# Solved blocks packed and spread on VectorE, adaptive vectors summed on VectorE

## The chip, the cores and the metric

One core of a Trainium2 chip. The time of a run is what the device takes for one execution, in microseconds (us). Engines: TensorE (PE), VectorE (DVE), ScalarE (ACT), GpSimd (POOL) and SyncE (SP), which issues all the DMAs told of here. Each engine runs its own list of instructions in order and waits on semaphores for the others.

## What is computed

One layer of a hybrid diffusion block over 256 latent and 256 context tokens of width 1024. A normalised input, scaled and shifted by a conditioning vector, goes through one combined projection; branch A is a spatial-gating MLP, branch B a gated DeltaNet in both directions; both are merged, projected and added; then a grouped top-2 mixture of 16 experts follows. Two places matter here.

```python
def ada_params(cond, w_ada, b_ada):
    return jnp.split(jax.nn.silu(cond) @ w_ada + b_ada, 6, axis=-1)

m = jnp.where(strict, jnp.einsum('bhnik,bhnjk->bhnij', k_beta, k) * decay, 0.0)
t_inv = lax.linalg.triangular_solve(eye + m, eye, left_side=True, lower=True, unit_diagonal=True)
u_val = t_inv @ (v * beta)
w_key = t_inv @ (k_beta * jnp.exp(gc)[..., None])

def step(s, inp):
    a_n, u_n, w_n, qd_n, kd_n, gt_n = inp
    v_new = u_n - w_n @ s
    o_n = qd_n @ s + a_n @ v_new
    s = s * gt_n + jnp.einsum('bhck,bhcv->bhkv', kd_n, v_new)
    return s, o_n
```

The adaptive vectors are a product of one row of 1024 with a matrix of 1024 x 6144, and the inverse is that of a unit lower triangular matrix per head, direction and tile of tokens.

## The kernel before

**Pairs and tiles.** The 8 heads are worked in 4 pairs, i = 0 to 3. A pair has 2 heads, 2 directions and 4 tiles of 128 tokens: 16 triangular problems of 128 x 128. While pair i is inverted and scanned, the projections of the next pair j = i + 1 are made (convolution channels C0 to C5, dense columns D0 to D6, gate columns Z0 and Z1); beside the last pair it is branch A (PA0 to PA7). The work of all engines is ordered by hand, one list for each engine.

**The stream of weight halves.** Weights come as halves of 512 KB: SP's half(n) (L621) loads half n into one of HRING = 4 buffers and first waits until half n - 4 is released. A weight half is rounded by ScalarE (high, L1164) and the rest subtracted by VectorE (low, L1734), which releases it; ahead(m) does this two halves ahead of the one now used, and ScalarE's and VectorE's lists each have it. SP's after_split(m) (L668) loads the half that takes the buffer of half m + 2. An adaptive vector (numbers 0 to 7, 512 columns each) comes as four quarters of such halves; a quarter is released by the sum or product made of it (ada_taken). The order of all halves is fixed by PLAN. Call the quarters of vector 2i a0 to a3 and those of 2i + 1 b0 to b3. For pairs 0 to 2 the order of loading, which runs two halves ahead of PLAN's places, is C4 C5 a0-a3 D3 Z0 b0-b3 D4 Z1 D5 D6, then C0 and C1 of the next pair; beside the last pair it is PA5 a0-a3 PA6 PA7 b0-b3 PB0 (with a, b for vectors 6 and 7).

**The block solve.** VectorE writes the triangular matrices; SP's move_rows (L690) puts their rows into a DRAM tensor, move_blocks (L695) reads back the 16 x 16 diagonal blocks, and GpSimd inverts them (solve_blocks, L963). SP's move_solved (L702) stores the inverses, and their transposes, into the diagonals of two large DRAM tensors that were zeroed once, t_dram and u_dram; move_inverse (L708) reads corners of 64 columns from them, zeros and all, into u_by_lane and t_by_lane. write_zeros (L680) does the zeroing in 12 DMAs of 172 KB, and zeroes rows of the experts too.

**The levels.** TensorE's level_p (L2708) waits for u's corners, level_up (L2726) for t's. VectorE's masks (L1887) and updates come between, then quarter_p, quarter_up, last_p, last_copy (L1919), and place_last on ScalarE: the whole inverse.

**The scan.** Per pair four steps: TensorE solved(t), ScalarE new_value(t) (L1341), TensorE state_sum(t), VectorE new_state(t) (L1935, L1940), TensorE key_state(t + 1), VectorE residual(t + 1) (L1927), with state_query and step_out (L1948) beside them. TensorE fills between with the products of D3 to D6, Z0 and Z1 of the next pair; low and ahead of these halves stand between VectorE's steps. o_scale (L1349) and decay_exp then begin the next pair.

**The adaptive vectors.** TensorE's ada_chunk (L2872) multiplies quarters as they land, two per call, into bank 3; ScalarE copies the bank (ada_copy, L1384), TensorE adds the partial rows and the bias (ada_fold, L2886), ScalarE copies the row (L1392) and SP stores it.

Of the kernel before, what the change touches and what calls it, by code (L numbers as in the profile page):

```python
# [20 lines left out]
P = 128  # L21
D = 1024
# [73 lines left out]
def block_kernel(nc, x, c, ctx, c_ctx, w_ada, b_ada, norm1_g, norm2_g, w_in, a_ln_g, a_w_s, a_b_s,  # L96
# [3 lines left out]
    with stack:  # L100
# [17 lines left out]
        fold_bias = sb("fold_bias", [P, 8])  # L118
# [181 lines left out]
        ada_part = lane_part(26)  # L300
        ada_sums, ada_bias = ada_part[0:97, :], ada_part[P - 8:P, :]
        zeros = lane_part(6)
        blocks, raw_blocks = lane_part(12)[:, 0:256], lane_part(12)[:, 256:512]
# [34 lines left out]
        def tokens(at):  # L338
# [13 lines left out]
            "landed_ctx landed_x landed_small landed_gate landed_bias bias_room landed_conv landed_ab ident_ready squares_ready power_ready "  # L352
# [5 lines left out]
            "scores_ready decay_exp intra_exp m_ready intra_ready landed_zero landed_rows landed_blocks blocks_solved landed_solved "  # L358
            "p_sum p_masked up_sum u_updated inverse_placed "
            "step_ready ks_sum r_ready qs_sum qs_copied vnew_sum vnew_copied intra_sum o_part "  # L360
# [5 lines left out]
            "ada_taken ada_copied ada_folded ada_stored "  # L366
# [29 lines left out]
        row_dram, t_dram, u_dram = [nc.dram_tensor(name, (PROBLEMS * (P // BLOCK) * STRIP,), F32).ap()  # L396
                                    for name in ("problem_rows", "inverse_turned", "inverse")]
# [10 lines left out]
        def corner(t, b):  # L408

            whole = t.rearrange("(m x) -> m x", m=PROBLEMS)  # L410
            return whole[:, 4 * b * STRIP:4 * b * STRIP + 64 * P].rearrange("m (r k) -> r m k", r=64)[:, :, 0:HALF_BLOCK]
# [50 lines left out]
        for j in range(1, PAIRS):  # L462
# [67 lines left out]
        def dense_bank(n):  # L530
            return bank[2 if n > 24 and n % 2 else 3][:, 0:256]

# [84 lines left out]
        def _(sp):  # L617
# [46 lines left out]
            def store_ada(m):  # L664
                sp.wait_ge(s["side_copied"], SIDE_AT["ada", m] + 1)
                load(ada_dram[m * N:m * N + N].unsqueeze(0), ada_part[0:1, :], s["ada_stored"])
# [13 lines left out]
            def write_zeros():  # L680
                sp.wait_ge(s["ident_ready"], 3)
                for t in (t_dram, u_dram):
                    flat = t.rearrange("(p x) -> p x", p=P)
                    for n in range(6):
                        load(flat[:, n * 344:(n + 1) * 344], zeros[:, 0:344], s["landed_zero"])
# [9 lines left out]
            def move_blocks():  # L695
                sp.wait_ge(s["landed_rows"], 64 * i + 64)
                if i == 0:
                    sp.wait_ge(s["landed_zero"], 320)
# [46 lines left out]
            write_zeros()  # L745
            after_split(CHAN_AT[j, 2])
# [11 lines left out]
            sp.wait_ge(s["bias_room"], 1)  # L758
# [2619 lines left out]
```

## Time and profile before

| | |
|---|---|
| median of three runs | 862.99 us (861.13 to 866.02) |
| the profiled execution | 862.04 us |
| its span in the trace | 860.3 us |
| mean granted clock of TensorE | 0.973 |
| TensorE, VectorE, ScalarE, GpSimd busy | 775.3, 523.3, 423.0, 197.5 us |

The profile is of one execution. The span runs from the first instruction to the last; 1.7 us of the execution's time lie outside it. A granted clock of 1.00 is 2.4 GHz, 0.50 is 1.2 GHz. In the rows, L2512 is the line of the helper that issues nearly all matrix products, so the tile names tell the work apart. "[x <-y]" is the engine's idle time ahead of an instruction and what ended it; "issue" stands where the profile shows no waiting. A row of SP's is the time of issuing, not of the transfer.

### The profile page before, as it was taken

Reading aid. Unit: us, or ns where it says so; the run is one execution under the profiler, and the core shown is the slowest. Engines: PE = TensorE matmul, PEld = TensorE weight load, DVE = VectorE, ACT = ScalarE, POOL = GpSimd, SP = SyncE. Lnnn points to the kernel's source line nnn. Section 1 sums busy time; section 2 is a strip of 40 time slices with the busy share of each in tenths; the row PEclk is TensorE's granted clock in tenths of the full one; section 3 lists DMA queues with packets and bytes.
Section 4 is the critical chain, followed back from the end, with each engine's and each line's share of the span. In section 5 each row is a group of like instructions: output and inputs, shape, how many; then the busy total and the mean of one; then the engine's idle time right before and its main releaser. Section 6 shows DMA issues by size and latency. Waiting matters only on the chain.

```text
span 860.3 us, 15936 instructions
## 1 busy us (share of the span) xinstructions
PE 775.3 (90%) x6396; PEld 634.1 (74%) x6396; DVE 523.3 (61%) x780; ACT 423.0 (49%) x749; POOL 197.5 (23%) x362
## 2 busy tenths in 40 slices
PE   3998997999979999799779898998999999999975
PEld 1678886799858997599768778887777777687631
DVE  1488585457843578445564446668977675786143
ACT  3476653448425484245822445465666565673101
POOL 3003261103801137022230103011241223212201
PEclk9999998999989999899988999999999999999998
DMA  9969469535695366844867558863889999999992
GB/s 312 290 204 270 118 163 209 152 87 138 171 202 135 86 170 151 217 124 128 273 134 184 175 148 261 346 259 113 299 347 420 408 420 420 417 418 366 419 418 118
DMA packets 182021, 208.37 MB, mean 242 GB/s; under 512 B 50212, under 2 KB 155341, under 8 KB 169017
## 3 DMA queue, kind: packets, MB, share of 16 engines
q1 hardware_dynamic: 179833, 203.28, 72.8%
q0 software_dynamic: 2112, 4.04, 1.2%
q8 instruction: 52, 0.85, 0.4%
q14 instruction: 24, 0.20, 0.1%
HBM read 190.64 MB, written 20.22 MB: 245 GB/s over the span
## 4 chain that ended last, share of the span: by engine, by line
PE 59%; DMA 12%; DVE 10%; POOL 7%; issue 5%; ACT 4%; SPq 2%; POOLq 0%; ACTq 0%; DVEq 0%
PE bank L2512 57%; DMA raw<-in_w_e_dram 5%; POOL lane L980 3%; POOL lane L978 2%; SPq L619 2%; DVE w_lo L2197 2%; DMA half_raw<-in_w_in_dram 2%; PE bank L2515 2%; DMA lane<-problem_rows 2%; DMA problem_rows<-lane 1%; DMA raw<-in_w_ada_dram 1%; DVE chan L1833 1%; DVE half_lo L1737 1%; ACT lane L1292 1%; DMA mix_raw<-in_a_w_s_dram 1%
## 5 line engine op out<-in xcount | busy, mean ns | idle before, releaser
L2512 PE MATMUL bank<-hT,half_hi 128*128 128x256 f32 (+1 forms) x1024 | 226.6, 316 | 8.5 <-issue 4.8
L2512 PEld LDWEIGHTS bank<-hT,half_hi 128*128 128x128 f32 x1024 | 164.7, 189 | 24.5 <-issue 8.7
L2512 PE MATMUL bank<-hT,half_lo 128*128 128x256 f32 (+1 forms) x512 | 158.3, 309 | 0.0
L1737 DVE TENSOR_TENSOR half_lo<-half_raw,half_hi 128x1024 fp32r<-128x1024 f32 x88 | 108.3, 1231 | 50.3 <-ACT half_hi L1169 49.4
L2197 DVE TENSOR_TENSOR w_lo<-raw,w_hi 128x2048 fp32r<-128x2048 f32 x36 | 88.2, 2458 | 46.8 <-ACT w_hi L1602 46.8
L1169 ACT CAST half_hi<-half_raw 128x1024 fp32r<-128x1024 f32 x88 | 91.9, 1048 | 41.2 <-PE bank L2512 22.4
L2512 PEld LDWEIGHTS bank<-lane 64*64 64x64 f32 (+3 forms) x1968 | 82.0, 149 | 33.5 <-issue 19.6
L2512 PE MATMUL bank<-lane 64*64 64x64 f32 (+3 forms) x1968 | 90.3, 239 | 16.6 <-issue 12.7
L2512 PEld LDWEIGHTS bank<-hT,half_lo 128*128 128x128 f32 x512 | 97.1, 190 | 7.2 <-issue 1.9
L1602 ACT CAST w_hi<-raw 128x2048 fp32r<-128x2048 f32 x36 | 68.7, 1909 | 34.6 <-PE bank L2512 19.9
L1833 DVE SCALAR_TENSOR_TENSOR chan<-bank,conv_col,chan 128x508 f32<-128x508 f32 (+3 forms) x96 | 63.2, 658 | 10.3 <-ACT chan L1240 7.7
L955 POOL TENSOR_TENSOR lane<-v_nat,key_gates 128x256 f32<-128x256 f32 x32 | 25.1, 789 | 177.4 <-DVE lane L1935 156.2
L2512 PE MATMUL bank<-w_hi,window 128*128 128x512 f32 x192 | 63.6, 399 | 1.6 <-DVE w_lo L2197 1.6
L2512 PE MATMUL bank<-w_lo,window 128*128 128x512 f32 x192 | 62.0, 397 | 0.2 <-DVE w_lo L2197 0.2
L2512 PE MATMUL bank<-raw,narrow_window 128*64 128x256 f32 x448 | 51.8, 382 | 4.1 <-DMA raw<-in_w_e_dram 4.0
L2512 PEld LDWEIGHTS bank<-raw,narrow_window 128*64 128x64 f32 x448 | 31.0, 137 | 22.3 <-issue 4.6
L2197 DVE TENSOR_TENSOR w_lo<-raw,w_lo 128x2048 fp32r<-128x2048 f32 x18 | 42.5, 2363 | 5.9 <-ACT w_lo L1602 5.9
L2512 PEld LDWEIGHTS bank<-w_hi,window 128*128 128x128 f32 x192 | 36.1, 188 | 12.7 <-issue 4.5
L2512 PEld LDWEIGHTS bank<-w_lo,window 128*128 128x128 f32 x192 | 35.8, 188 | 8.7 <-DVE w_lo L2197 0.6
L1602 ACT CAST w_lo<-raw 128x2048 fp32r<-128x2048 f32 x18 | 34.4, 1910 | 11.0 <-PE bank L2512 7.7
L2512 PE MATMUL bank<-w_lo,act_hi 128*128 128x512 f32 x108 | 37.0, 397 | 0.0
L1068 POOL CAST window<-hT 128x2048 fp32r x8 | 19.5, 2434 | 58.0 <-PE bank L2512 37.2
(386 smaller groups left out, 1352.6 us busy)
## 6 DMA issues: line engine op xcount, KB each, us to landing
raw<-in_w_e_dram SPq DMA_DIRECT2D x96, 1024.0 KB, 10.8
half_raw<-in_w_in_dram SPq DMA_DIRECT2D x64, 512.0 KB, 5.0
half_raw<-in_w_ada_dram SPq DMA_DIRECT2D x32, 512.0 KB, 4.7
raw<-in_w_ada_dram SPq DMA_DIRECT2D x8, 1024.0 KB, 11.5
dense<-staged SPq DMA_DIRECT2D x32, 128.0 KB, 4.6
half_raw<-in_w_proj_a_dram SPq DMA_DIRECT2D x8, 512.0 KB, 5.9
half_raw<-in_w_proj_b_dram SPq DMA_DIRECT2D x8, 512.0 KB, 5.0
half_raw<-in_w_out_dram SPq DMA_DIRECT2D x8, 512.0 KB, 6.3
```

The source lines that it names most:

```text
L619: sp.dma_start(dst, src).then_inc(done, 16)
L955: last = pool.tensor_tensor(v_beta[pos % 2][:, :, d, :], v_nat[i % 2][:, :, t, :], key_gates[i % 2][:, KEY_BETA, t, :, d:d + 1].to_broadca ...
L978: own.after(pool.tensor_tensor(product_, y[:, k + 1:, k:k + 1].to_broadcast([P, rows_, cols_]), x[:, k:k + 1, 0:k + 1].to_broadcast([P, ro ...
L980: own.after(pool.tensor_tensor(x[:, k + 1:, 0:k + 1], x[:, k + 1:, 0:k + 1], product_, ALU.subtract))
L1068: pool.tensor_copy(window[q % 2][:, :, :, :], hT[:, :, :, bass.ds(at, P)].bitcast(F32))\
L1169: act.copy(half_hi[m % HBUF][:, :], half_raw[n % HRING][:, :]).then_inc(s["half_high"], 1)
L1602: act.copy(e_hi[k % WBUF][:, :], slots[n % SLOTS_AHEAD][:, :]).then_inc(s["hi_ready"], 1)
L1737: dve.tensor_tensor(half_lo[m % HBUF][:, :], half_raw[n % HRING][:, :], half_hi[m % HBUF][:, :].bitcast(F32), ALU.subtract).then_inc(s["ha ...
L1833: ins = dve.scalar_tensor_tensor(out=y[:, :, a:b], in0=ps[:, :, a + o:b + o], scalar=conv_col[:, CONV_KIND[n // 2], 2 * j + n % 2, tap:tap ...
L2197: dve.tensor_tensor(e_lo[k % WBUF][:, :], slots[n % SLOTS_AHEAD][:, :], e_hi[k % WBUF][:, :].bitcast(F32), ALU.subtract)\
L2512: return nc.tensor.matmul(dst, lhsT, rhs, start=start, stop=stop)
L2515: return nc.tensor.transpose(dst, src, ident[0:rows_, 0:rows_])
```

## The change

The inverses of the diagonal blocks are stored packed, u's two stores first, and read back in two loads in the layout [128 rows, 16 problems, 16 columns]; VectorE multiplies each with a mask that puts every block at its place and zeros elsewhere (corners, a tensor_tensor of 128 x 1024, two per pair). level_p and level_up wait for these instead of the loads. The twelve zeroing DMAs of t_dram and u_dram go. SP issues the two loads right behind the stores.

The adaptive vectors are summed on VectorE: a quarter holds 256 rows of the matrix, two to a partition, and two scalar_tensor_tensor instructions of 128 x 512 add them, weighted, to ada_sum, which starts from the bias. One product of TensorE with a column of ones (ada_fold) sums over the partitions. The order of loading becomes C4 C5 D3 Z0 a0-a3 D4 Z1 b0-b3 D5 D6; beside the last pair it stays as it was. ScalarE's place_last moves ahead of the rounding of D4, and the rounding of D5 behind the copy of D4.

```diff
...
         def add_ada(m, early=0):
-            SIDE_AT["ada", m] = len(SIDE_AT)
             PLAN.insert(len(PLAN) - early, m)
...
             add_chan(j, 3)
-            add_ada(2 * (j - 1) + 0)
             add_chan(j, 4)
             add_chan(j, 5)
-            add_ada(2 * (j - 1) + 1)
+            add_ada(2 * (j - 1) + 0)
             add_dense(3 + 7 * (j - 1) + 3)
             add_z(j, 0)
+            add_ada(2 * (j - 1) + 1)
             add_dense(3 + 7 * (j - 1) + 4)
...
             def move_solved():
                 sp.wait_ge(s["blocks_solved"], i + 1)
                 for d in range(DIRS):
-                    for to, done in ((u_dram if d else t_dram, solved_blocks), (t_dram if d else u_dram, turned_blocks)):
-                        load(diagonal(to, d), square(done[64 * d:64 * d + 64, :]), s["landed_solved"])
+                    load(by_solver(u_dram, d), (solved_blocks if d else turned_blocks)[64 * d:64 * d + 64, :], landed_inverse[0])
+                for d in range(DIRS):
+                    load(by_solver(t_dram, d), (turned_blocks if d else solved_blocks)[64 * d:64 * d + 64, :], landed_inverse[1])
 
             def move_inverse():
-                sp.wait_ge(s["landed_solved"], 64 * i + 64)
-                for at_, (to, source) in enumerate(((u_by_lane, u_dram), (t_by_lane, t_dram))):
-                    for b in range(2):
-                        load(to[64 * b:64 * b + 64, :, :, :].rearrange("p d m n -> p (d m) n"), corner(source, b), landed_inverse[at_])
+                for at_, (to, source) in enumerate(((u_packed, u_dram), (t_packed, t_dram))):
+                    sp.wait_ge(landed_inverse[at_], 48 * i + 32)
+                    load(to, by_rows_of(source), landed_inverse[at_])
...
                 move_solved()
-                ada_halves(2 * i + 0, 0, 2)
                 move_inverse()
-                ada_halves(2 * i + 0, 2, 4)
                 after_split(CHAN_AT[j, 4])
+                after_split(CHAN_AT[j, 5])
+                ada_halves(2 * i + 0, 0, 4)
+                load_ada_bias(2 * i + 1)
+                spill(3 + 7 * i + 3)
+                after_split(DENSE_AT[3 + 7 * i + 3])
+                after_split(Z_AT[j, 0])
                 store_ada(2 * i + 0)
-                after_split(CHAN_AT[j, 5])
-                after_ada(2 * i + 1)
+                ada_halves(2 * i + 1, 0, 1)
+                load_ada_bias(2 * i + 2)
+                spill(3 + 7 * i + 4)
+                ada_halves(2 * i + 1, 1, 3)
+                spill(3 + 7 * i + 5)
+                ada_halves(2 * i + 1, 3, 4)
+                after_split(DENSE_AT[3 + 7 * i + 4])
+                after_split(Z_AT[j, 1])
                 store_ada(2 * i + 1)
...
                 place_quarters()
                 place_corners()
+                place_last()
                 ahead(DENSE_AT[3 + 7 * i + 3])
-                place_last()
                 dense_copy(3 + 7 * i + 3)
                 new_value(0)
                 ahead(Z_AT[j, 0])
                 z_parts(0)
+                ada_line_copy(2 * i + 0)
                 new_value(1)
+                dense_copy(3 + 7 * i + 4)
                 ahead(DENSE_AT[3 + 7 * i + 4])
-                dense_copy(3 + 7 * i + 4)
...
+            def corners():
+                shape = [P, PROBLEMS, HALF_BLOCK // BLOCK, BLOCK]
+                for at_, (to, packed) in enumerate(((u_by_lane, u_packed), (t_by_lane, t_packed))):
+                    dve.wait_ge(landed_inverse[at_], 48 * i + 48)
+                    dve.tensor_tensor(to.rearrange("p d m (j c) -> p (d m) j c", c=BLOCK), packed.unsqueeze(2).to_broadcast(shape),
+                                      block_at[:, 0:4].unsqueeze(1).unsqueeze(3).to_broadcast(shape), ALU.mult)\
+                        .then_inc(s["corners_ready"], 1)
...
+            def ada_steps(m, first, last):
+
+                for c in range(first, last):
+                    n = ADA_AT[m] + c
+                    dve.wait_ge(half_landed[n % HRING], 16 * (n // HRING + 1))
+                    if c == 0:
+                        dve.wait_ge(s["landed_bias"], 16 * m + 16)
+                        if m:
+                            dve.wait_ge(s["ada_folded"], m)
+                    else:
+                        dve.wait_ge(s["ada_taken"], 4 * m + c)
+                    rows_of = two(half_raw[n % HRING])
+                    own.after(dve.scalar_tensor_tensor(out=ada_sum[:, :], in0=rows_of[:, 0, :], scalar=cols[:, 2 * c:2 * c + 1],
+                                                       in1=(ada_sum if c else ada_first)[:, :], op0=ALU.mult, op1=ALU.add))
+                    dve.scalar_tensor_tensor(out=ada_sum[:, :], in0=rows_of[:, 1, :], scalar=cols[:, 2 * c + 1:2 * c + 2],
+                                             in1=ada_sum[:, :], op0=ALU.mult, op1=ALU.add).then_inc(s["ada_taken"], 1)
...
                 taps(4)
                 ahead(CHAN_AT[j, 4])
+                corners()
                 silu(4)
                 masks()
...
                 last_copy()
+                ada_steps(2 * i + 0, 0, 4)
                 ahead(DENSE_AT[3 + 7 * i + 3])
                 new_state(0)
                 residual(1)
                 ahead(Z_AT[j, 0])
                 z_gate(0)
+                ada_steps(2 * i + 1, 0, 1)
                 new_state(1)
+                residual(2)
                 ahead(DENSE_AT[3 + 7 * i + 4])
-                residual(2)
+                ada_steps(2 * i + 1, 1, 2)
                 z_gate(1)
+                ada_steps(2 * i + 1, 2, 3)
                 new_state(2)
                 ahead(Z_AT[j, 1])
                 step_out(2)
                 residual(3)
+                ada_steps(2 * i + 1, 3, 4)
                 step_out(3)
...
             branch_a(3)
+            ada_steps(6, 0, 3)
             new_state(0)
             branch_a(4)
             residual(1)
+            ada_steps(6, 3, 4)
             ahead(PA_AT[4])
+            ada_steps(7, 0, 2)
             new_state(1)
             branch_a(5)
             residual(2)
             ahead(PA_AT[5])
+            ada_steps(7, 2, 4)
             new_state(2)
...
                 solved(0)
                 z_part(0, 0)
                 state_sum(0)
+                ada_fold(2 * i + 0)
                 z_part(0, 1)
...
                 solved(3)
+                ada_fold(2 * i + 1)
                 intra_sum(3)
...
```

## Rows read from the trace of the kernel before

**Rows 1.** the page, parts 1 and 4: busy times; the chain by engine.
```profile
PE 775.3 (90%) x6396; PEld 634.1 (74%) x6396; DVE 523.3 (61%) x780; ACT 423.0 (49%) x749; POOL 197.5 (23%) x362
...
PE 59%; DMA 12%; DVE 10%; POOL 7%; issue 5%; ACT 4%; SPq 2%; POOLq 0%; ACTq 0%; DVEq 0%
```

**Rows 2.** chain of waits, first pair, 129 to 161 us: start, us, what.
```profile
129.92 0.61 SPq L619
...
140.81 2.54 issue
143.35 3.68 PE bank L2512 x64
...
159.17 1.83 issue
161.00 28.50 PE bank L2512 x264
```

**Rows 3.** SP's queue, first pair: start, us of issuing, engine line op out<-in.
```profile
135.14 2.65 SPq L619 DMA_DIRECT2D lane<-inverse  x2
137.83 3.36 SPq L619 DMA_DIRECT2D lane<-inverse_turned  x2
```

**Rows 4.** DMA issues, whole span: xcount, KB each, median us to landing.
```profile
lane<-inverse SPq DMA_DIRECT2D x8, 256.0 KB, 7.0
...
lane<-problem_rows SPq DMA_DIRECT2D x8, 64.0 KB, 3.1
...
inverse<-lane SPq DMA_DIRECT2D x8, 64.0 KB, 3.4
```

**Rows 5.** landing of the six half loads, first pair's scan, 160 to 196 us.
```profile
DMA to landing us min/median/max: 4.1/4.5/5.4
```

**Rows 6.** stretches: length, PE busy, granted clock, DMA share, GB/s.
```profile
142.30:149.10 6.80, 5.75 (x94) 0.50 1.16 266
159.20:193.00 33.80, 31.07 (x285) 1.00 0.38 100
262.90:268.50 5.60, 3.92 (x42) 0.70 0.62 149
```

**Rows 7.** timeline of the first pair: levels, scan, end of scan; [idle before].
```profile
152.11 1.92 PE L2512 MATMUL bank<-half_raw,cond_pad 128*32 128x512 f32 x16
...
158.55 0.69 DVE L1919 COPY lane<-bank 128x512 f32<-128x512 f32 x1 [0.89 <-PE bank L2512]
...
160.88 1.05 ACT L1169 CAST half_hi<-half_raw 128x1024 fp32r<-128x1024 f32 x1
...
165.73 0.59 ACT L1341 COPY lane<-bank 128x512 f32<-128x512 f32 x1 [0.52 <-PE bank L2512]
...
170.37 1.12 DVE L1927 SCALAR_TENSOR_TENSOR lane<-bank,key_gates,lane 128x128 f32<-128x128 f32 x4 [1.64 <-PE bank L2512]
...
185.27 0.68 DVE L1948 TENSOR_TENSOR lane<-lane,bank 128x512 f32<-128x512 f32 x1
...
193.98 0.31 ACT L1349 ACTIVATE sq_junk<-lane 128x128 bf16<-128x128 f32 x1
```

**Rows 8.** timeline, DVE, two additions behind each other elsewhere.
```profile
570.85 0.69 DVE L2204 SCALAR_TENSOR_TENSOR arena_hi<-lane,arena_hi 128x512 f32<-128x512 f32 x1
571.57 0.69 DVE L2206 TENSOR_TENSOR arena_hi<-arena_hi,ada_vec 128x512 f32<-128x512 f32 x1
```

**Rows 9.** timeline of the last pair: DVE, and PE at its levels' start.
```profile
451.42 1.23 DVE L1737 TENSOR_TENSOR half_lo<-half_raw,half_hi 128x1024 fp32r<-128x1024 f32 x1 [0.28 <-ACT half_hi L1169]
...
453.80 1.01 PE L2512 MATMUL bank<-lane 64*64 64x64 f32 x14 [4.61 <-issue]
...
497.08 1.21 DVE L1737 TENSOR_TENSOR half_lo<-half_raw,half_hi 128x1024 fp32r<-128x1024 f32 x1
502.74 1.12 DVE L1940 SCALAR_TENSOR_TENSOR lane<-lane,gates,bank 128x128 f32<-128x128 f32 x4 [4.44 <-PE bank L2512]
```

**Rows 10.** the stage in which the zeros are written, all engines.
```profile
57.00:80.00 23.00, 21.67 (x155) 19.60 (x154) 22.40 (x44) 15.80 (x45) 4.21 (x7) 1.00 1.01 318
```

More of the change, by code:

```diff
@@ L299, in block_kernel @@
         o_turned = lane_part(10).rearrange("p (h n) -> p h n", h=2)
-        ada_part = lane_part(26)
-        ada_sums, ada_bias = ada_part[0:97, :], ada_part[P - 8:P, :]
+        ada_line = lane_part(26)[0:1, :]
+        ada_sum, ada_first = [at(name, LANE_AT + (54 + 2 * n) * KB, [P, N]) for n, name in enumerate(("ada_sum", "ada_first"))]
         zeros = lane_part(6)
+        u_packed, t_packed = [lane_part(15)[:, 256 * n:256 * n + 256].rearrange("p (q c) -> p q c", c=BLOCK) for n in range(2)]
         blocks, raw_blocks = lane_part(12)[:, 0:256], lane_part(12)[:, 256:512]
@@ L406, in lane_rows, with by_solver, by_rows_of @@
             return tiles.rearrange("p (m d n) -> p m d n", d=DIRS, n=P)[:, :, d, :]
-        def corner(t, b):
-            whole = t.rearrange("(m x) -> m x", m=PROBLEMS)
-            return whole[:, 4 * b * STRIP:4 * b * STRIP + 64 * P].rearrange("m (r k) -> r m k", r=64)[:, :, 0:HALF_BLOCK]
+        def by_solver(t, d):
+            return t.rearrange("(n x) -> n x", n=P)[64 * d:64 * d + 64, :]
+        def by_rows_of(t):
+            return t.rearrange("(q p c) -> p q c", q=PROBLEMS, p=P)
         def diagonal(t, d):
@@ L681, in write_zeros @@
                 sp.wait_ge(s["ident_ready"], 3)
[L682 to L685, printed above, removed]
                 for n in range(LISTED // P):
@@ L810, in _ @@
             move_solved()
+            move_inverse()
             after_split(DENSE_AT[28])
@@ L1724, in _ @@
             dve.wait_ge(s["cols_copied"], 1)
-            own.mark(dve.tensor_tensor(fold_bias[:, :], ident[:, P - 8:P], fold[:, 0:1].to_broadcast([P, 8]), ALU.add))
+            own.after(dve.tensor_reduce(block_at[:, 4:12], ident[:, :].rearrange("p (j c) -> p j c", c=BLOCK), AX, ALU.add))
+            own.mark(dve.tensor_tensor(block_at[:, 0:4], block_at[:, 4:8], block_at[:, 8:12], ALU.add))
             dve.wait_ge(s["cols_ready"], 1)
@@ L1888, in masks @@
                     dve.wait_ge(s["p_sum"], i * P_SUMS + (half + 1))
+                    if half:
+                        dve.wait_ge(s["corners_ready"], 2 * i + 2)
                     dve.tensor_tensor(p_half[:, 4 * half:4 * half + 4, :, :], four_by_two(4 + half),
@@ L2146, in _ @@
             ahead(DENSE_AT[30])
+            corners()
             masks()
@@ L2870, in mix @@
                     ins.then_inc(s["mix_sum"], 1)
-            def ada_chunk(m, first=0, last=4):
-                if first == 0:
-                    pe.wait_ge(s["side_copied"], SIDE_AT["ada", m])
-                for c in range(first, last):
-                    n = ADA_AT[m] + c
-                    if c % 2 == 0:
-                        pe.wait_ge(half_landed[n % HRING], 16 * (n // HRING + 1))
-                        pe.wait_ge(half_landed[(n + 1) % HRING], 16 * ((n + 1) // HRING + 1))
-                    for kk in range(2):
-                        kc = 2 * c + kk
-                        r = 32 * (kc % 4)
-                        ins = mm(bank[3][r:r + 32, :], cond_pad[:, kc, :], two(half_raw[n % HRING])[:, kk, :], kc < 4, kc >= 4)
-                    ins.then_inc(s["ada_taken"], 1)
-            def ada_fold(m):
-                pe.wait_ge(s["ada_copied"], m + 1)
-                if m == 0:
-                    pe.wait_ge(s["landed_bias"], 16)
-                mm(bank[3][0:1, :], fold_bias[:, m:m + 1], ada_part).then_inc(s["ada_folded"], 1)
+            def ada_fold(m):
+                if m < 2 * (PAIRS - 1) and m % 2 == 0:
+                    pe.wait_ge(s["taps_done"], j * 6 + 5)
+                elif m < 2 * (PAIRS - 1):
+                    pe.wait_ge(s["ksq_ready"], j * 4 + 4)
+                else:
+                    pe.wait_ge(s["side_copied"], len(SIDE_AT))
+                if m:
+                    pe.wait_ge(s["ada_line_ready"], m)
+                pe.wait_ge(s["ada_taken"], 4 * m + 4)
+                mm(ada_bank(m)[0:1, :], ones[:, 0:1], ada_sum[:, :]).then_inc(s["ada_folded"], 1)
             def branch_a(m):
```

79 lines of the change are left out of this document (29 added, 50 removed).

## The prediction

> **What bounds the kernel now.** First the page's busy times and its chain by engine: TensorE is busy 775.3 of 860.3 us and carries 59% of the chain, VectorE 61% busy with 10% [rows 1]. So room on VectorE is there on average, and the question is where TensorE waits. The chain of waits of the first pair of heads shows one such place: the solve's results leave at 129.92, and level_p, the first work on them, begins at 143.35; before it TensorE stands 2.54 us [rows 2]. SP's queue says what lies between: four stores, two weight halves, then the corners, u's loads issued from 135.14 and t's from 137.83, in 6.0 us of issuing [rows 3]; these transfers of 256 KB take 7.0 us to land [rows 4]. Behind the levels it is different: from 161.00 TensorE runs 28.50 us without a gap [rows 2], 31.07 of 33.80 us busy at a granted clock of 1.00 [rows 6]. There nothing late is forgiven: VectorE, ScalarE and loads are hidden, but with little to spare.
>
> Times below are those of the first pair; the next two repeat it. I call T the end of last_copy, 158.55 + 0.69 = 159.24, and R the start of residual(1), 170.37, 11.13 after T [rows 7].
>
> **The block round trip: a gain.** Before, from 129.92 to 143.35 are 13.4 us. After, the two stores of u go first. A 64 KB store in short runs now takes 3.4 us to land [rows 4]; its rows are now 1 KB whole, so I take 3.3 for the two, u in memory at 133.2. Its load has 2048 runs of 64 bytes. The nearest row is the read of the diagonal blocks, 1024 such runs: 3.1 to land [rows 4]. For twice the runs I take 4.0, between 3.1 and the 7.0 of today's corner loads: 137.2. VectorE then spreads it; it may first finish a weight half's subtraction, which ends near 137.6. A tensor_tensor of 128x1024 takes 1.23 [rows 9]; no row has its stepped mask, so up to twice that. level_p begins at 137.6 + 1.22 + a hand-over = 138.95, that is 4.4 earlier; t's spread hides beneath it. Bounds: with the load at 7.0 and the spread at 2.4, level_p begins at 142.7, 3.8 worse; with the load at 3.1 it is 0.9 better at most, if the half before it comes as early. silu(4) and the masks stand behind the spread on VectorE, at about their old times. I carry **-4.3** to T. The last pair gains nothing: VectorE's split ahead of the spreads ends at 452.65 there, u's spread at 453.9, and level_p begins at 453.80 today [rows 9].
>
> **TensorE's adaptive products: nothing.** The sixteen products in the levels (1.92 us [rows 7]) lie beneath VectorE's updates, those before them beside waits for the corners. What stays is one column sum per vector.
>
> **VectorE's sums.** Each quarter costs two scalar_tensor_tensor of 128x512 that wait for one another. Such a pair starts 570.85 and 571.57 elsewhere: 0.72 apart [rows 8], so 1.45 a quarter; 32 quarters are 46 us, the eight spreads 10. VectorE has that room; the cost is in who waits. In the ring of four halves a quarter's buffer is now freed by its sum, and not by TensorE ahead of the scan. In the new order (D3, Z0, a0 to a3, D4, Z1, b0 to b3, D5, D6) D4's load waits for a0's sum, D5's for b0's, D6's for b1's; SP's later issues queue behind each wait. Isolated loads of this stage land in 4.1 to 5.4, mostly about 4.4 [rows 5].
>
> - T to R: a0 is done at T+1.45, D4 lands at T+5.85, and ScalarE rounds it (1.05 [rows 7]) until T+6.9. That rounding now stands ahead of the copy of D3 and of new_value(0), which ends near T+7.9 and ended at 165.73 + 0.59, T+7.1 [rows 7]. 0.8 late; the column sum, put between state_sum and z_part, adds about 0.4 beyond new_state's cover. **+1.2**, bounds 0 and 2.
> - R to step_out(2): residual(1) 1.12, a subtraction 1.22, a gate 0.4, then b0's 1.45: R+4.1. D5 lands at R+8.5, is rounded (1.05) and subtracted (1.22) by R+10.8, b1 follows until R+12.2, only then D6 goes out, lands at R+16.6 and is split at R+18.8. step_out(2), behind that subtraction, was at 185.27, R+14.9 [rows 7]: **+3.9**. Without a wait it would be 0; with each load 0.9 dearer, 5.7.
> - step_out(2) to the pair's end (o_scale at 193.98 [rows 7]): b3's sum and the second column sum stand before intra_sum(3), partly beneath TensorE's dense products: **+0.5**, 0 to 1.5.
>
> Together -4.3 + 1.2 + 3.9 + 0.5 = +1.3 per pair, +3.9 for three.
>
> **The last pair.** The quarters of b7 go out each behind a sum or a split; the second behind a6's last sum, which makes new_state(1) 2.3 late by the same reckoning (sum 1.45, load 4.4, sum 1.45 against the hole there). The fourth goes behind PA7's subtraction, today until 498.3, so near 500.5, lands at 504.9, and new_state(2), today at 502.74, waits for the sum until 506.4 [rows 9]: 3.7 late. TensorE's products behind branch A give back about 1: **+2.7**, 0 to 3.7.
>
> **The zeros.** Twelve stores of 172 KB go. Where they are written VectorE is busy 22.40 of 23.00 us [rows 10]; it covers them, **-0.3** (0 to -0.5). In the levels the smaller loads also leave the queues emptier: counted in the landings.
>
> **Sum:** 3.9 + 2.7 - 0.3 = +6.3 on the profiled execution's 862.0: 868.3. That execution lies 0.95 under the median of the three runs, 862.99; I leave the sum unshifted.
>
> **Rivals.**
> 1. *Faster: the scan hides its loads.* The place is D6's split: it decides at R+14.9. If it comes by then, 3.9 and 0.5 vanish, and with D4 on time most of 1.2. A pair then keeps 4.3 less about 0.6 of column sum, -3.7; three give -11.1, and the last pair's price falls to some 1.5: 862.0 - 11.1 + 1.5 - 0.3 = 852. For it: half loads of 512 KB move while the DMA share in the scan is 0.38 [rows 6], and VectorE does each sum in a hole. Against it: two loads and two sums stand in series, and the fastest landing, 4.1, saves only 0.6 of 3.9.
> 2. *No net change: the clock stays up.* From 142.3 to 149.1 the granted clock is 0.50, the 1.2 GHz level, following TensorE's wait for the corners; level_p takes 3.68 in it [rows 2, 6]. If the shorter wait leaves it at 2.4 GHz, level_p takes about half, 1.8 less, and 0.2 to 0.5 more comes behind it: 2.0 to 2.3 a pair, 868.3 - 6.5 = 862. "TensorE: Matmul & The Clock Gate" in the Trainium skill (What's actually happening) says the same of direction: a TensorE left idle is put back to half rate. By that rule the sum would be 862, and this trace's fall agrees with it. Against it: several shorter waits remain ahead of level_p.
> 3. *Slower still: the clock falls in the scan.* In the second pair a stall inside the dense products is followed by 0.70 from 262.9 to 268.5 [rows 6], though the first pair's of 1.83 [rows 2] is not. The new waits for D4, D5 and D6 are of 1.7 to 3 us. One or two falls a pair, at 0.3 of 5.6 us or 1.7 each, give +5 to +10: 873 to 878.
>
> **How the numbers follow.** Forecast (866 to 872) 0.40, rival 1 0.21, rival 2 0.23, rival 3 0.16. A measurement here can tell about 0.5%, 4.3 us. Faster takes rival 1 and a little of rival 2, 0.24; slower takes forecast and rival 3 less a part that a cheaper landing pulls under 867, 0.52; the same, 0.24. The range goes from rival 1's better than middle, 853, to rival 3's upper part, 877. The likeliest case alone is 864 to 873.
>
> **What would show it.** Right: level_p near 139 in the first pair; ScalarE's rounding of D4 waiting on a DMA ahead of new_value(0); VectorE waiting for D6's rounding ahead of step_out(2), TensorE's 28.50 us run broken in three places; decay_exp of the second pair about 1 us later than before. Wrong: TensorE's run unbroken (rival 1), or level_p at 2 us (rival 2), or a clock under 1.00 in the scan (rival 3). A spread far dearer than 1.2, or u landing after 140, would show in level_p's start.

## The result and the profile after

The changed kernel takes 880.31 us in the median of 4 runs (874.90 to 882.88), the kernel before 863.59 us in 4; the ratio is 1.019 (95% interval 1.016 to 1.023), some 17 us slower. The profiled execution is the shortest of the four, 874.90 us, with a span of 873.2.

The page of the changed kernel, busy times and the chain by engine, beside [rows 1]:

```profile
PE 768.5 (88%) x6268; PEld 638.5 (73%) x6268; DVE 577.9 (66%) x853; ACT 418.6 (48%) x741; POOL 196.3 (22%) x362
...
PE 57%; DVE 18%; DMA 15%; ACT 4%; issue 3%; POOL 1%; SPq 1%; POOLq 0%; DVEq 0%; ACTq 0%
```
TensorE has 7 us less to do, VectorE 55 more (523.3 before), as the change says. The chain shows what that means: VectorE's share rose from 10% to 18%, the loads' from 12% to 15%, GpSimd's fell from 7% to 1%.

The chain of waits of the first pair (start, us, what), beside [rows 2]:

```profile
138.89 1.23 issue
140.12 2.10 PE bank L2549 x64
...
156.37 4.76 DMA half_raw<-in_w_in_dram
...
162.22 0.38 ACT staged L1291
...
162.64 6.05 PE bank L2549 x42
...
172.79 5.22 DMA half_raw<-in_w_in_dram
...
181.81 4.17 DMA half_raw<-in_w_in_dram
...
188.97 5.51 PE bank L2549 x38
```
The pair starts 1.4 us later here than before (decay_exp at 93.50 and 92.07). That is no effect of the change: the same start is at 91.31 in the second trace of this kernel below, and between 91.3 and 94.6 in all twelve traces. In this trace TensorE loses the time between 26.3 and 31.7, where three groups of products take 1.87, 2.15 and 1.67 us, and 1.05, 1.18 and 1.07 before; why they do is open. level_p begins at 140.12 (143.35 before) behind an idle time of 1.23 and takes 2.10 instead of 3.68. Then TensorE's unbroken 28.50 us are gone. In their place stand three loads on the chain, issued at 156.37, 172.79 and 181.81: the halves D4, D5 and D6, each of which waits for a sum.

TensorE's granted clock in stretches of the changed kernel (stretch, length, PE busy, clock, DMA share, GB/s), beside [rows 6]:

```profile
142.30:149.10 6.80, 4.60 (x162) 1.00 0.27 80
154.89:196.10 41.21, 35.07 (x290) 0.97 0.50 147
398.00:409.00 11.00, 9.96 (x63) 0.84 0.60 156
```
The first levels, at half rate before, now run at 1.00; the scan, at 1.00 in the first pair before, no longer does, and in the third pair's end (398 to 409) it is 0.84. The last two levels ahead of last_copy go the other way. The stretches that hold them in pairs 0 to 2, first in the changed kernel, then in the kernel before:

```profile
149.30:154.20 4.90, 4.45 (x163) 0.66 0.02 3
255.00:260.00 5.00, 4.83 (x133) 0.50 0.02 3
360.00:365.00 5.00, 4.77 (x160) 0.50 0.02 3
...
154.60:158.50 3.90, 3.75 (x147) 1.00 1.00 267
257.90:262.00 4.10, 3.94 (x161) 1.00 1.05 270
363.00:367.20 4.20, 4.01 (x165) 1.00 1.04 277
```
Where the adaptive products stood, TensorE now waits for VectorE's updates, 1.72 and 0.74 us in the first pair, and what follows runs near half rate: in the first pair the last 96 products of 32x32 and the 32 of 64x64 ahead of last_copy take 1.60 and 1.97 us, 1.23 and 1.15 before. The three kernels of the table below that keep the adaptive products on TensorE (before, blocks_only, blocks_early) have 1.15 for these 32 in all three pairs; the others have 1.97 to 2.49 wherever the trace shows the 32 as one row.

VectorE in the last pair of the changed kernel (timeline; idle time ahead of an instruction, and its releaser, in brackets), beside [rows 9]:

```profile
503.80 0.75 DVE L2055 SCALAR_TENSOR_TENSOR ada_sum<-half_raw,cols,ada_first 128x512 f32<-128x512 f32 x1 [3.48 <-PE bank L2549]
...
506.90 1.12 DVE L1949 SCALAR_TENSOR_TENSOR lane<-lane,gates,bank 128x128 f32<-128x128 f32 x4
...
516.42 0.75 DVE L2055 SCALAR_TENSOR_TENSOR ada_sum<-half_raw,cols,ada_sum 128x512 f32<-128x512 f32 x1 [2.52 <-DMA half_raw<-in_w_ada_dram]
...
517.88 1.12 DVE L1949 SCALAR_TENSOR_TENSOR lane<-lane,gates,bank 128x128 f32<-128x128 f32 x4
```
new_state(1) starts at 506.90, behind two sums that began only after a wait of 3.48 for TensorE; new_state(2) starts at 517.88, behind a sum that waited 2.52 for a load.

From the starts of decay_exp, last_copy, residual(1), step_out(2) and o_scale in each trace a pair can be cut into four stages: up to T (end of last_copy), T to R (start of residual(1)), R to step_out(2), and from there to o_scale. The last columns are the mean of pairs 0 to 2 whole (from decay_exp to the next pair's) and the last pair up to o_scale. All in us; the first three rows are the two kernels and the changed one in a second trace, the others the experiments below.

| kernel | to T | T to R | R to step_out(2) | to o_scale | pairs 0 to 2 | last pair | median |
|---|---|---|---|---|---|---|---|
| before | 67.5 | 11.4 | 14.9 | 8.7 | 103.7 | 111.2 | 863.6 |
| after | 61.5 | 13.9 | 19.4 | 9.4 | 105.4 | 119.3 | 880.3 |
| after_again | 61.8 | 14.6 | 19.3 | 10.5 | 107.4 | 117.5 | 877.6 |
| blocks_only | 67.6 | 9.9 | 14.9 | 8.7 | 102.3 | 111.7 | 861.7 |
| sums_only | 64.9 | 14.1 | 19.4 | 9.9 | 109.5 | 113.9 | 886.5 |
| fold6_early | 61.4 | 13.8 | 19.2 | 10.4 | 106.0 | 116.0 | 875.8 |
| scan_early | 62.1 | 11.5 | 14.9 | 9.1 | 98.8 | 117.7 | 852.2 |
| last_early | 61.5 | 14.5 | 19.4 | 10.4 | 107.0 | 112.5 | 870.9 |
| both_early | 61.7 | 11.8 | 14.9 | 9.2 | 98.8 | 113.4 | 848.2 |
| blocks_early | 63.8 | 11.9 | 14.9 | 8.7 | 100.5 | 110.6 | 851.5 |
| d4_early | 61.6 | 11.9 | 19.4 | 9.4 | 103.5 | 117.9 | 868.8 |
| d5_d6_early | 61.0 | 13.8 | 14.9 | 9.5 | 100.4 | 121.7 | 862.7 |

Stages of the traces shift from one execution to the next, mostly by up to a microsecond or two (the start of a pair is ScalarE's, and loads vary). T to R of the first pair differs by 3.7 between the two traces of the changed kernel, and the last pair lies between 117.5 and 121.7 in the five traces that have it as in the change. So a stage is compared where it moves by more, or where it repeats.

### The profile page after: what moved, and what is told of

Read it like the earlier page. It is cut to its first block, busy times and chain, and to the rows that moved or that the text cites. A ratio compares the mean times of both kernels' runs of the same rounds, so it can differ in the third digit from the quotient of the medians.

```text
span 873.2 us, 15758 instructions
## 1 busy us (share of the span) xinstructions
PE 768.5 (88%) x6268; PEld 638.5 (73%) x6268; DVE 577.9 (66%) x853; ACT 418.6 (48%) x741; POOL 196.3 (22%) x362
## 4 chain that ended last, share of the span: by engine, by line
PE 57%; DVE 18%; DMA 15%; ACT 4%; issue 3%; POOL 1%; SPq 1%; POOLq 0%; DVEq 0%; ACTq 0%
PE bank L2549 55%; DMA raw<-in_w_e_dram 5%; DMA half_raw<-in_w_in_dram 5%; DVE chan L1832 3%; DVE half_lo L1736 3%; PE bank L2552 2%; DVE w_lo L2234 2%; DMA raw<-in_w_ada_dram 1%; DMA half_raw<-in_w_out_dram 1%; ACT half_hi L1177 1%; DVE ada_sum L2055 1%; SPq L625 1%; DVE ada_sum L2057 1%; DVE lane L1907 1%; DMA mix_raw<-in_a_w_s_dram 1%
## 5 line engine op out<-in xcount | busy, mean ns | idle before, releaser
L2549 PE MATMUL bank<-hT,half_hi 128*128 128x256 f32 (+1 forms) x1024 | 229.8, 320 | 12.6 <-ACT z_raw L1284 6.9
L2549 PEld LDWEIGHTS bank<-hT,half_hi 128*128 128x128 f32 x1024 | 167.9, 193 | 29.0 <-ACT z_raw L1284 7.9
L2549 PE MATMUL bank<-hT,half_lo 128*128 128x256 f32 (+1 forms) x512 | 160.3, 313 | 0.0
L2234 DVE TENSOR_TENSOR w_lo<-raw,w_hi 128x2048 fp32r<-128x2048 f32 x36 | 88.5, 2466 | 46.6 <-ACT w_hi L1600 46.6
L2549 PEld LDWEIGHTS bank<-lane 64*64 64x64 f32 (+3 forms) x1968 | 82.4, 150 | 31.7 <-issue 14.2
L2549 PEld LDWEIGHTS bank<-hT,half_lo 128*128 128x128 f32 x512 | 99.1, 194 | 5.3
L2549 PE MATMUL bank<-w_lo,window 128*128 128x512 f32 x192 | 62.1, 397 | 0.2 <-DVE w_lo L2234 0.2
L966 POOL TENSOR_TENSOR lane<-v_nat,key_gates 128x256 f32<-128x256 f32 x32 | 22.6, 710 | 170.9 <-DVE lane L1944 142.2
```

Source lines behind the costliest of these rows:

```text
L966: last = pool.tensor_tensor(v_beta[pos % 2][:, :, d, :], v_nat[i % 2][:, :, t, :], key_gates[i % 2][:, KEY_BETA, t, :, d:d + 1].to_broadca ...
L2234: dve.tensor_tensor(e_lo[k % WBUF][:, :], slots[n % SLOTS_AHEAD][:, :], e_hi[k % WBUF][:, :].bitcast(F32), ALU.subtract)\
L2549: return nc.tensor.matmul(dst, lhsT, rhs, start=start, stop=stop)
```

## The experiments

Each set ran beside its own runs of the kernel before: medians 862.2, 861.9 and 862.4 us. They agree, so kernels of different sets are compared directly.

**after_again.** The changed kernel, unaltered.

> The changed kernel once more, unaltered, as the measure for the others of this set and for a second trace. The first trace was of the shortest of its runs (874.9, the median 880.3). Theory: the chains are the same in every run (12 to 14 us over the kernel before in the four pairs), and what differs between runs is where TensorE's clock falls to half rate behind the new waits in the scan: then a trace of a run near 880 has the same gaps and some 5 us more of stretches under a granted clock of 1.00. Rival: the loads land later in those runs: then the three waits for D4, D5 and D6 are longer by 1 to 2 us a pair.

877.62 us, 1.021 (1.015 to 1.026) of the kernel before; the trace is of an execution of 876.61. The gaps repeat, with one difference: the first pair's T to R takes 17.5 us and not 13.8. TensorE at D3's second part, and the clock behind it:

```profile
162.24 0.79 PE L2549 MATMUL bank<-hT,half_hi 128*128 128x256 f32 x2 [3.67 <-ACT staged L1291]
```
```profile
162.24:168.27 6.03, 6.03 (x23) 0.53 0.53 170
```
D4's load took 5.87 us here (4.76 in the first trace), TensorE stood 3.67 us (1.73 there), and the next 6.03 us ran at 0.53. Both halves of the expectation have a part: the longer landing makes 1.1 of the longer wait, and the fallen clock adds to it behind the wait. The rest comes from TensorE being done earlier: its work between T and this wait takes 5.2 us here, at a granted clock of 0.92, and 6.0 in the first trace, at 0.77. From step_out(2) to o_scale it is 10.5 in all three pairs, against 8.9, 8.9 and 10.5 in the first trace; the granted clock of this stage is 0.84 wherever it takes 10.5, and 1.00 where it takes 8.9.

**blocks_only and sums_only.** The two parts apart. blocks_only is the kernel before with move_solved, move_inverse, corners and the waits on them as in the change, and the twelve zeroing stores gone; D3's and Z0's loads still stand between the two moves. In VectorE's list:

```diff
                 taps(4)
-                ahead(CHAN_AT[j, 4])
+                corners()
                 silu(4)
                 masks()
+                ahead(CHAN_AT[j, 4])
                 ahead(CHAN_AT[j, 5])
```

> The kernel before with the packed blocks alone: stores, two loads and VectorE's spreads of the change (the spreads ahead of the weight half's subtraction, which goes behind the masks; D3 and Z0 still issued between stores and loads), no zeroing; the adaptive vectors stay TensorE's products. Theory (the loss is all in the sums): level_p starts 4 us earlier in pairs 0 to 2, at full clock, the scan runs as before, each pair is about 5.5 to 6 us shorter, the last one within 1: 863 - 17 = 846, at most 850. Rival (the shorter wait is given back behind, in waits of the scan that were hidden): 855 to 863.

861.71 us, 0.999 (0.996 to 1.002): no gain. The masks come 2.9 us earlier, last_copy does not. TensorE between level_p and quarter_p (timeline), SP's queue beside it:

```profile
141.11 2.08 PE L2527 MATMUL bank<-lane 64*64 64x64 f32 x64 [1.57 <-issue]
...
147.37 1.07 PE L2527 MATMUL bank<-half_raw,cond_pad 128*32 128x512 f32 x8
152.03 1.94 PE L2527 MATMUL bank<-half_raw,cond_pad 128*32 128x512 f32 x8 [3.60 <-DMA half_raw<-in_w_ada_dram]
153.90 1.08 PE L2527 MATMUL bank<-lane 32*32 32x32 f32 x64
```
```profile
132.92 1.34 SPq L624 DMA_DIRECT2D lane<-inverse  x1
...
146.21 0.38 SPq L624 DMA_DIRECT2D half_raw<-in_w_ada_dram  x1
```
The row at 152.03 is the answer: the products of b2 and b3 wait 3.60 us for b3's load, issued at 146.21, when Z0 is subtracted, and quarter_p stands behind them. What the earlier corners gave was given back at a load that had been on time because the corners were late. Two things make it late now: my own move of D3's subtraction behind the masks puts it 1.1 us later, and it takes 5.7 us to land, 3.7 before; why it takes longer no run shows. So this kernel did not measure the blocks alone, and blocks_early below tries again.

sums_only is the changed kernel with move_solved, move_inverse, corner loads and zeros of the kernel before, and no spreads.

> The changed kernel with the old way of the solved blocks (strips of zeros, corners loaded, no spreads), and all of the sums on VectorE. Theory (two parts that add): this loses what the blocks gain, 5.8 a pair in three pairs, less 1 in the last: 880 + 16 = 896, 892 to 899. Rival (the parts overlap, the sums' waits would hide part of the old transfer): 882 to 888.

886.50 us, 1.028 (1.022 to 1.034): 6 to 9 us above the changed kernel and not 16. The rival is nearer. To T it takes 64.9, 2.6 less than the kernel before although the corners travel the old way. The cause stands in SP's queue: here no weight halves are issued between the stores and the corner loads. From the first store of the inverses to level_p it takes, as a mean of pairs 0 to 2, 14.0 us before, 10.8 in this kernel, 12.1 in blocks_only (packed, the halves still between) and 8.5 in the changed kernel. So taking the halves out is worth 3.2 to 3.6, and packing 1.9 to 2.3. To T the packed blocks add 3.4, since level_p runs at full clock with them (2.08) and mostly at half rate here (3.13, 3.68, 3.68). In the last pair it is the other way round: with packed blocks level_p waits for VectorE's spread, 13.5 behind the first store (13.4 before), and here, without a spread, it begins after 10.6. That is a large part of why the last pair takes 113.9 here and 117.5 or more where packed blocks and this order of sums stand together.

**fold6_early.** One line of TensorE's list in the last pair.

```diff
             solved(1)
+            ada_fold(6)
             branch_a(5)
             state_sum(1)
-            ada_fold(6)
```

> The changed kernel with one line moved: in the last pair TensorE's column sum of vector 6 stands right behind solved(1) and no longer behind branch A's fifth block and state_sum(1). VectorE's first sum of vector 7 waits for that column sum, because both vectors use one buffer, and new_state(1) stands behind two such sums. Theory (this wait is most of the last pair's loss of 8): VectorE starts the sums at about 500.5 and not at 503.8, new_state(1) starts at about 503.5 and not at 506.9: 3.4 less, 876.9 against 880.3. Rival (the sums' own time on VectorE, or the load of the fourth quarter, sets the last pair's end): under 1 less.

875.80 us (after_again in the same set 877.62), the last pair 116.0 against 117.5: under half of the 3.4. (That 875.80 lies close to the expected 876.9 is luck: that figure was reckoned from the first set's 880.3, and within this set the difference is 1.8, less than a measurement here can tell.) The chain of waits shows what took its place:

```profile
499.10 0.76 DVE ada_sum L2057
...
500.29 3.16 DMA ada_first<-in_b_ada_dram
...
503.53 0.76 DVE ada_sum L2055
...
506.63 1.13 DVE lane L1949 x4
```
Vector 7's bias: SP issues it behind the load that waits for vector 6's last sum, at 500.29, and it is there 3.16 us later, where the sums begin. From the start of residual(1) to the first sum it is 6.3 us here (497.28 to 503.53) and was 7.2 (496.61 to 503.80): a wait was taken away and the next one stood 0.9 us behind it.

**scan_early, last_early, both_early.** The sums moved, and SP's loads of D5 and D6 with them; no work added or removed. scan_early:

```diff
...
                 after_split(DENSE_AT[3 + 7 * i + 3])
+                ada_halves(2 * i + 1, 0, 1)
+                load_ada_bias(2 * i + 2)
                 after_split(Z_AT[j, 0])
+                ada_halves(2 * i + 1, 1, 2)
                 store_ada(2 * i + 0)
-                ada_halves(2 * i + 1, 0, 1)
-                load_ada_bias(2 * i + 2)
...
+                ada_steps(2 * i + 0, 0, 1)
                 last_copy()
-                ada_steps(2 * i + 0, 0, 4)
+                ada_steps(2 * i + 0, 1, 4)
                 ahead(DENSE_AT[3 + 7 * i + 3])
                 new_state(0)
+                ada_steps(2 * i + 1, 0, 1)
                 residual(1)
                 ahead(Z_AT[j, 0])
                 z_gate(0)
-                ada_steps(2 * i + 1, 0, 1)
+                ada_steps(2 * i + 1, 1, 2)
                 new_state(1)
                 residual(2)
                 ahead(DENSE_AT[3 + 7 * i + 4])
-                ada_steps(2 * i + 1, 1, 2)
                 z_gate(1)
```

> The changed kernel with the sums of pairs 0 to 2 moved ahead, all of them still VectorE's: a0 ahead of last_copy, b0 ahead of residual(1), b1 ahead of new_state(1); SP issues D5 and D6 ahead of the loads that wait for later splits. Same work on every engine. Theory (the loss is loads that wait for sums, three in series, and TensorE's clock falling behind them): step_out(2) comes 15 us after residual(1) as in the kernel before and not 19.4, T to R shrinks by 1.5 to 3, a pair takes 97 to 99 us and not 105 to 110: 858 or less, about 855. Rival (VectorE's added work sets the pace wherever it stands): residual(1) and new_state(1) are late by the 1.6 us of a sum each, a pair gains under 2: 872 to 876.

852.21 us, 0.987 (0.982 to 0.992): 25 us under after_again. R to step_out(2) is 14.9 again. VectorE in the first pair of this kernel, b0 and b1 in their new places:

```profile
163.22 0.80 DVE L2056 SCALAR_TENSOR_TENSOR ada_sum<-half_raw,cols,ada_first 128x512 f32<-128x512 f32 x1 [0.44 <-DMA ada_first<-in_b_ada_dram]
164.05 0.98 DVE L2058 SCALAR_TENSOR_TENSOR ada_sum<-half_raw,cols,ada_sum 128x512 f32<-128x512 f32 x1
165.55 1.13 DVE L1937 SCALAR_TENSOR_TENSOR lane<-bank,key_gates,lane 128x128 f32<-128x128 f32 x4 [0.51 <-PE bank L2551]
...
168.06 0.74 DVE L2056 SCALAR_TENSOR_TENSOR ada_sum<-half_raw,cols,ada_sum 128x512 f32<-128x512 f32 x1
168.84 0.75 DVE L2058 SCALAR_TENSOR_TENSOR ada_sum<-half_raw,cols,ada_sum 128x512 f32<-128x512 f32 x1
170.26 1.12 DVE L1950 SCALAR_TENSOR_TENSOR lane<-lane,gates,bank 128x128 f32<-128x128 f32 x4 [0.68 <-PE bank L2551]
```
b0 ends at 165.03 and residual(1) still waits 0.51 for TensorE; b1 ends at 169.59 and new_state(1) still waits 0.68. The sums lie in holes of VectorE's; the same 1.6 us, placed three steps of the list later, had put a load, a rounding and a subtraction on the path. TensorE's run behind D4 is whole again in the chain of waits:

```profile
159.47 27.25 PE bank L2551 x216
```
last_early puts vector 6's sums ahead of new_state(0), its column sum behind state_sum(0), the bias of vector 7 behind the first quarter, and the last quarter behind residual(3):

```diff
-            ada_halves(6, 0, 4)
+            ada_halves(6, 0, 1)
             load_ada_bias(7)
+            ada_halves(6, 1, 4)
...
-            ada_steps(6, 0, 3)
+            ada_steps(6, 0, 4)
             new_state(0)
             branch_a(4)
             residual(1)
-            ada_steps(6, 3, 4)
             ahead(PA_AT[4])
             ada_steps(7, 0, 2)
             new_state(1)
...
-            ada_steps(7, 2, 4)
+            ada_steps(7, 2, 3)
             new_state(2)
             step_out(2)
             branch_a(6)
             residual(3)
+            ada_steps(7, 3, 4)
```

> The changed kernel with the last pair's sums moved: vector 6 is summed whole ahead of new_state(0), its column sum follows state_sum(0), the bias of vector 7 is loaded behind the first quarter's sum and not the fourth's, the last quarter is summed behind residual(3). Theory (of the last pair's loss of 6 to 8, all is in three waits on VectorE: the column sum, the bias behind it, the fourth quarter's load): from the pair's start to o_scale 112 to 113 us and not 117.5 to 119.3, 872 to 874 in all. Rival (the sums' length): at best the 2 that the earlier column sum alone brought.

870.92 us, 1.010 (1.006 to 1.013); the last pair takes 112.5 against 117.5 to 119.3 and 111.2 before. Nearly all of its loss was these waits.

> The two kernels before this one together. Theory: their gains add, 846 to 852, faster than the kernel before by 10 or more. Rival: 868 to 872.

848.20 us, 0.981 (0.977 to 0.986): faster than the kernel before by 1.9%, with all that the change adds. blocks_early below, with the vectors still on TensorE, comes to 851.49, so most of this gain does not need the sums on VectorE. What they bring by themselves is not shown: both_early also has the halves out from between stores and loads, and blocks_early has not. The chain by engine of its page:

```profile
PE 63%; DVE 16%; DMA 12%; ACT 3%; issue 2%; POOL 1%; SPq 1%; POOLq 0%; DVEq 0%; ACTq 0%
```
**blocks_early.** blocks_only with D3's subtraction put back ahead of the spreads, and Z0's ahead of the masks, where the kernel before does not have it:

```diff
+                ahead(CHAN_AT[j, 4])
                 corners()
                 silu(4)
+                ahead(CHAN_AT[j, 5])
                 masks()
-                ahead(CHAN_AT[j, 4])
-                ahead(CHAN_AT[j, 5])
```

> The packed blocks alone, adaptive vectors on TensorE, now with D3's subtraction ahead of the spreads and Z0's ahead of the masks. In the first form of this kernel the masks came 2.5 to 3 us earlier than in the kernel before and last_copy did not: TensorE waited 3.6 us for the quarter b3 ahead of quarter_p, whose load goes out only when Z0 is subtracted. Theory: b3's load goes out about 2.5 to 3 us earlier, last_copy follows, 853 to 856. Rival (the load is late for another reason, or the subtraction ahead of the masks costs what it gives): 860 to 863.

851.49 us, 0.987 (0.982 to 0.992). SP's queue: b3's load goes out at 143.37.

```profile
132.62 1.58 SPq L624 DMA_DIRECT2D lane<-inverse  x1
...
143.37 0.38 SPq L624 DMA_DIRECT2D half_raw<-in_w_ada_dram  x1
```
To T it is 63.8, 3.7 less than before, and the scan is untouched. That load lands in 4.1 us here. So the packed blocks, with the loads behind them early too, are worth 1.3%; Z0's earlier subtraction is part of that, and the kernel before with this move alone was not run.

**d4_early and d5_d6_early.** scan_early's two parts: a0's sum alone moved ahead of last_copy, and everything but that.

> The changed kernel with a0's sum alone moved, ahead of last_copy in pairs 0 to 2, so that D4's load goes out about 1.5 us earlier. Theory (the wait for D4 has a length and, behind it, a price in TensorE's clock): T to R falls from 13.1 to 17.5 us to 11.5 to 12.5, the rest of a pair stays; 2 to 3 a pair, 7 in all, about 871. Rival (T to R is long because of the column sum and the four sums ahead of new_state(0)): under 1 a pair.

868.82 us, 1.010 (1.006 to 1.013): 9 less than after_again, from one sum in another place. T to R falls to 11.9 and the rest of the pair keeps its length.

> The changed kernel with b0's and b1's sums and SP's order as in the kernel with the scan's sums ahead, a0 left where it was. Theory: R to step_out(2) falls from 19.4 to 14.9, and with the wait for D6 gone the clock stays up behind it, step_out(2) to o_scale falls from 10.5 to 9; T to R stays at 13 to 17.5; 5 to 6 a pair, 17 in all, about 861. Rival (half rate comes with any wait and not with these): step_out(2) to o_scale stays at 10.5, about 865.

862.71 us, 1.000 (0.997 to 1.003): 15 less. R to step_out(2) is 14.9, and T to R keeps 13.8. Behind step_out(2) it is 9.5, between the 9 and the 10.5 that were set against each other. The granted clock there is 1.00 in all three pairs; more of TensorE's work falls into the stage (9.0 to 9.4 us busy, 7.9 in the pairs with 8.9). With the wait for D6 left in, the clock is 0.84 there in some pairs (one of three in the first trace and in d4_early, all in the second trace) and 1.00 in others. 9 and 15 make 24, and scan_early had 25.

## Why the prediction was wrong

The direction was right, the ways the time goes were those named, and the size was not: 868.3 us forecast, range 853 to 877, 880.3 measured. Step by step, against the first trace unless said otherwise:

- **The block round trip, -4.3.** The path was right: level_p begins 46.6 us behind the pair's start and 51.3 before, 4.7 earlier in the first pair (4.4 in the text). The transfer was mis-sized on the dear side: I took 4.0 us for the read of u, and it lands in at most 2.9 (the landings of the two stores of u and of its load; the largest bounds the load):

```profile
DMA to landing us min/median/max: 2.1/2.4/2.9
```
 VectorE's subtraction ahead of the spread decided instead, as the text allowed. And rival 2 came true beside the forecast: level_p at full clock, 2.10 instead of 3.68. The Trainium skill's rule ("TensorE: Matmul & The Clock Gate", What's actually happening) agrees in direction: 0.50 behind the wait of 2.54 us, 1.00 behind that of 1.23. To T the mean of the three pairs is -6.0. The text priced the whole trip and not its two parts; by the stores-to-level_p times under sums_only, more of it comes from the halves that no longer stand between stores and loads than from the packing.
- **TensorE's products, nothing.** That they lay beneath VectorE's updates was read right, but taking them out is not free: the last two levels run near half rate without them (1.60 and 1.97 us, 1.23 and 1.15 before), about 1.2 us dearer in the first pair. The text put this at nothing. No run takes out the products alone, but the fall stands in sums_only too, so it is not the packing's.
- **T to R, +1.2.** Measured +2.5, and +3.2 in the second trace. D4's load took 4.8 to 5.9 and not 4.4; the column sum lies on the path with its whole 1.0 and not 0.4, ahead of z_part; and TensorE's clock is down for part of it, with a granted clock of 0.90, 0.88 and 0.86 in the three pairs (1.00, 0.86 and 1.00 before), and 0.78 in the first pair of the second trace.
- **R to step_out(2), +3.9.** Measured +4.5, and d5_d6_early shows that the chain of two loads and two sums is its cause: without it 14.9, as before. Two quarters' sums start 1.63 apart (154.81 and 156.44), not 1.45.
- **To o_scale, +0.5.** +0.7 in the first trace, +1.8 in the second.
- **The last pair, +2.7.** This is the step that failed: +8.1, and +6.3 in the second trace, against bounds of 0 to 3.7. I had the load of the fourth quarter and missed the wait in front of it. Both vectors are summed in one buffer, so vector 7's first sum waits for vector 6's column sum, which stands in TensorE's list behind branch A's block and state_sum(1); and its bias stands in SP's queue behind vector 6's last sum. fold6_early and last_early show both: from last_copy to o_scale the last pair takes 36.3 us before, 41.5 to 44.5 in the six traces with the sums of the last pair in the order of the change, 40.7 in fold6_early and 35.9 in last_early. The wait was in the diff (a wait on ada_folded ahead of the first quarter), and the text priced the instruction and not its wait.
- **The zeros, -0.3.** From the taps beside which the zeros are written (VectorE at 53.94 before, 55.38 after) to the first decay_exp (92.07 and 93.50) it is 38.1 us in both traces: nothing, within the bounds given.

Of the 6.6 us between forecast and the first trace's 874.9, 5.4 are the last pair's. The other three pairs are 1.1 over the forecast in sum, and that this is so little is luck: 1.7 a pair too little gain to T was forecast, and 2.1 too little loss behind it. The later start of the first pair (1.4), what comes behind the last o_scale (-1.6) and the zeros (0.3) nearly cancel. What lies between that trace and the median of 880.3 is in untraced executions. The second trace shows where it can lie: pairs 0 to 2 are at +3.7 each there instead of +1.7, nearly all of it in T to R and behind step_out(2), where clock and landing vary. I had put a fallen clock in the scan into a rival of its own, at 0.16, against the forecast. It is no rival: it comes on top of the waits that the forecast itself adds, and its 5 to 10 us should have been in the forecast's own range, whose upper end was then too low. Likewise rival 2 and the forecast were not alternatives; the first levels gained their clock while the last ones and the scan lost theirs. And the range began at 853, although rival 1's own sum in it was 852.

Rival 1 asked for D6 by R + 14.9. With the sums moved it comes, in scan_early, and the pair gains 4.9 and not the 3.7 that I gave it. Nothing in VectorE's load stood against it, only the order of sums and loads.

What stays open: why the clock falls behind some of these waits and not behind others, why D4's load lands in 4.8 us in one execution and in 5.9 in another, and which of the untraced runs had a fallen clock where.

## What to carry to other kernels

When work moves to an engine that has room, price first what its instructions release, and only then its busy time. Here nine sums in pairs 0 to 2, some 15 us of VectorE (9 of 1.63), and the loads that they release decide over 25 us: in one order the scan keeps the length that it had before, in the other, a few steps later, each sum holds the buffer of a load that the next stage needs. Read every wait that a new instruction brings, and what stands ahead of its releaser in that engine's own list. A gain on one path shows in the time only when the next path is early too: the earlier blocks gave nothing until one more load was brought forward. And work that was hidden on TensorE can be missed when it goes: behind the gap that it leaves the granted clock fell.

## What was not expected of the hardware

A short transfer behind two weight halves takes as long as the old one. The read of u with 2048 runs of 64 bytes landed within 2.9 us in the first pair of the changed kernel, and in blocks_only, where SP issues two loads of 512 KB right ahead of it, in 6.8:

```profile
DMA to landing us min/median/max: 2.3/2.4/6.8
```
The loads of u over the whole span (xcount, KB each, median us to landing), the old corners in sums_only, where no halves go ahead of them, then the packed blocks in blocks_only and in the changed kernel:

```profile
lane<-inverse SPq DMA_DIRECT2D x8, 256.0 KB, 4.0
...
lane<-inverse SPq DMA_DIRECT2D x4, 128.0 KB, 6.6
...
lane<-inverse SPq DMA_DIRECT2D x4, 128.0 KB, 3.0
```
So of the 7.0 us that the corner loads took before [rows 4], 3.0 go with the halves ahead of them, and packing takes 1.0 off the 4.0 that are left.

A spread with a stepped mask of 16-element runs costs no more than a plain one: two of 128x1024 take 2.35 us together, 1.2 each, as the subtraction of that size [rows 9].

TensorE's clock falls behind a wait of 3.67 us in the first pair's scan of the second trace (0.53 above); in the first trace, where the wait at this place is 1.73, the products behind it keep their short times (0.50 for two of D3's, 0.79 in the second).
